# Attention C and D by query blocks: queries prepared three units ahead, a third bank for the maxima, shift rows turned a step later, and half of D's far masks added by TensorE

## What is computed

```python
# C: each chunk of 64 queries sees a band of keys (itself and two chunks back), with T5 bias and a sink
oc = chunk_band_prompt(qc, kc, vc, C_BACK_CHUNKS, bias_c, sinks)

# D: the 256 best keys of every query, chosen by an index score
_, sel = lax.top_k(score, topk)
s = jnp.einsum('bqhd,bqjd->bhqj', q, ks).astype(F32) * (q.shape[-1] ** -0.5) + bias   # T5 bias
s = jnp.where(valid[:, None], s, NEG_INF)
p = jax.nn.softmax(s, axis=-1).astype(vs.dtype)
o = jnp.einsum('bhqj,bqjd->bqhd', p, vs)
```

## Time and profile before

| | us |
|---|---|
| median of 3 runs (4599.81 to 4607.68) | 4602.56 |
| the profiled execution, its own time | 4597.78 |
| its span in the trace | 4596.0 |
| PE busy over the span | 3885.7 (85%) |
| DVE busy | 2402.1 (52%) |
| ACT busy | 1543.8 (34%) |
| POOL busy | 676.7 (15%) |
| main loop of C, from the trace (3298 to 3538) | 240 |
| main loop of D (3600 to 4330) | 730 |

### The profile page before, as it was taken

One profiled execution on the slowest core, in us unless ns is written; L12 is line 12 of the kernel. 1 busy time (PEld: TensorE's weight loads), 2 busy tenths in 40 slices (PEclk: granted clock), 3 DMA queues, 4 the chain that ended last, 5 costly groups with the idle time before them and its releaser, 6 DMA issues. The chain is left out here.

```text
span 4596.0 us, 52423 instructions
## 1 busy us (share of the span) xinstructions
PE 3885.7 (85%) x18001; PEld 2683.2 (58%) x18001; DVE 2402.1 (52%) x5162; ACT 1543.8 (34%) x2330; POOL 676.7 (15%) x408
## 2 busy tenths in 40 slices
PE   5999999978878999997988887789576578889798
PEld 3789989956655656566846433334344345555376
DVE  6211111157765444433310999999655677777522
ACT  3101001024433333333300777860233233333332
POOL 3100000022202111103400000000111432111133
PEclk9999999989998999998999898899788699999899
DMA  5222121143324332204411111011312101000243
GB/s 184 62 74 73 64 71 68 65 109 81 82 61 98 71 65 62 61 9 178 153 69 52 40 60 50 30 53 68 95 55 73 53 29 32 23 24 5 83 142 132
DMA packets 222647, 328.50 MB, mean 71 GB/s; under 512 B 22240, under 2 KB 129176, under 8 KB 221040
## 3 DMA queue, kind: packets, MB, share of 16 engines
q1 hardware_dynamic: 162768, 216.87, 16.8%
q10 hardware_dynamic: 54432, 91.91, 5.4%
q0 software_dynamic: 5216, 16.70, 1.7%
HBM read 214.42 MB, written 110.99 MB: 71 GB/s over the span
## 5 line engine op out<-in xcount | busy, mean ns | idle before, releaser
L2305 DVE TENSOR_SCALAR_CACHE_REDUCE cd_junk<-score,cd_thr 128x384 bf16<-128x384 f32 (+7 forms) x340 | 397.7, 1235 | 0.1
L1102 DVE TENSOR_REDUCE attB_mx<-attB_p_s 128x1 f32<-128x512 f32 (+2 forms) x360 | 211.3, 608 | 326.8 <-PE attB_p_s L949 209.8
L497 DVE COPY ab_stage<-ab_pA 128x256 f32<-128x256 f32 (+1 forms) x108 | 56.4, 522 | 601.1 <-PE ab_pA L466 571.5
L2345 ACT ACTIVATE cd_scratch<-score,cd_less 128x1664 bf16<-128x1664 f32 (+4 forms) x160 | 303.2, 1895 | 72.5 <-DVE cd_less L2324 67.0
L369 PE MATMUL cd_pA<-hT_cd,cd_W 128*128 128x512 f32 (+1 forms) x640 | 263.9, 577 | 74.0 <-ACT cd_stage L2451 61.5
L464 PE MATMUL ab_pA<-ab_W_hi,h_hi 128*128 128x256 f32 x1088 | 309.1, 284 | 3.3 <-PE ab_pA L466 3.2
L465 PE MATMUL ab_pA<-ab_W_lo,h_hi 128*128 128x256 f32 x1088 | 308.0, 283 | 0.0
L466 PE MATMUL ab_pA<-ab_W_hi,h_lo 128*128 128x256 f32 x1088 | 307.9, 283 | 0.0
L1575 PE MATMUL attD_p_o<-attD_pt,attD_v 128*65 128x512 f32 x548 | 296.4, 623 | 0.3
L1014 PE MATMUL attB_p_o<-attB_pt,attB_v 128*65 128x512 f32 (+3 forms) x656 | 287.5, 527 | 0.0
L495 ACT ACTIVATE ab_stage<-ab_pA 128x256 f32<-128x256 f32 (+1 forms) x108 | 50.0, 463 | 697.9 <-PE ab_pA L466 667.5
(11 more groups left out here) (378 smaller groups left out, 9294.0 us busy)
## 6 DMA issues: line engine op xcount, KB each, us to landing
t_qg<-cd_stage ACTq DMA_DIRECT2D x74, 256.0 KB, 2.0
ab_W_raw<-in_w_ab SPq DMA_DIRECT2D x17, 1024.0 KB, 5.8
mix_o<-t_o SPq DMA_DIRECT2D x34, 512.0 KB, 4.3
t_q<-ab_stage ACTq DMA_DIRECT2D x40, 256.0 KB, 2.0
t_k<-ab_stage ACTq DMA_DIRECT2D x40, 256.0 KB, 2.0
attA_raw<-t_k SPq DMA_DIRECT2D x16, 640.0 KB, 7.3
attA_raw<-t_q SPq DMA_DIRECT2D x16, 640.0 KB, 12.6
attB_raw<-t_k SPq DMA_DIRECT2D x16, 640.0 KB, 7.4
```

What stands on the lines that cost most here:

```text
L1102: nc.vector.tensor_reduce(out, src, AX.X, ALU.max).then_inc(s_free, 1)
L2305: nc.vector.tensor_scalar(junk[n % 2][:, 0:w], sc[n][:], T[:, n:n + 1], None, op, ALU.add, accum_out=cnt[:, n:n + 1]).then_inc(counted, 1)
L2345: nc.scalar.activation(scratch[:, 0:w], sc[n][:], ACT.Sign, bias=less[:, k:k + 1], accum_out=cnt[:, n:n + 1]).then_inc(signed, 1)
```

## The change

The plan and the instruction lists of `attention_by_blocks` change in four ways.

- **Queries ahead.** ACT's `round_queries(b)` and POOL's `prepare(b)` move from one step before the block's first fills to `due[u - 3]`, three units ahead. DVE's `split_queries(b)` gets a place of its own, two steps behind that (`split_at`). The `near_t` part of `prepare` becomes `add_near(b)`, at `due[u]`. The buffers (`NQ` = 3, two `q_raw`) stay.
- **Banks.** `p_s` has 3 banks (a fill waits for the reader of the bank three uses back) and `p_t` 2: `scores(c + 2)` waits for the reader of chunk `c`, before it was chunk `c - 1`.
- **Rows.** `shift_row(u)` and `keep_row(u)` move from `due[u] + 1` to `due[u] + 2`, and within a step ahead of masks and fills.
- **Masks by PE.** In D, chunks with an even key tile that is not one of the two nearest (128 of 306) get their mask by a third matmul into `p_t` (identity by the turned mask, 512 columns of bf16). ACT takes their exponent straight from `p_t`; DVE does nothing for them. `by_dve` and `biased` count the rest.

```diff
+        self.by_dve = [t >= self.chunks[self.chunks_of[u][-1]][1] - 1 or t % 2 == 1 for u, t in self.chunks]
+        self.biased = [sum(self.by_dve[:c + 1]) for c in range(len(self.chunks))]
...
-            self.rows_at[due[u] + 1].append(u)
+            self.rows_at[due[u] + 2].append(u)
...
-                self.blocks_at[max(begin - 1, 0)].append(b)
-        self.early_blocks = sorted({self.units[u][0] for u in self.early})
+                if b not in self.early_blocks:
+                    self.blocks_at[max(due[u - 3], 0)].append(b)
+                    self.split_at[max(min(due[u - 3] + 2, begin - 1), 0)].append(b)
+                    self.near_at[due[u]].append(b)
...
-        p_s = [ps(f"p_s{k}") for k in pair]
-        p_t = [ps(f"p_t{k}") for k in range(3)]
+        p_s = [ps(f"p_s{k}") for k in range(3)]
+        p_t = [ps(f"p_t{k}") for k in pair]
...
-            if g >= 2:
-                last = plan.order[g - 2]
+            if g >= 3:
+                last = plan.order[g - 3]
...
-                    if c >= 3:
-                        pe.wait_ge(t_biased, c - 2)
+                    if c >= 2 and plan.by_dve[c - 2]:
+                        pe.wait_ge(t_biased, plan.biased[c - 2])
+                    elif c >= 2:
+                        pe.wait_ge(exped, c - 1)
...
-                    nc.tensor.matmul(out, lo[:, ks], q_b[s][:, hs, :], start=False, stop=True).then_inc(t_done, 1)
+                    done = nc.tensor.matmul(out, lo[:, ks], q_b[s][:, hs, :], start=False, stop=plan.by_dve[c])
+                    if not plan.by_dve[c]:
+                        pe.wait_ge(mask_kept, plan.masks_before[b + 1])
+                        done = nc.tensor.matmul(out, identb[:], msk_t[b % 2][:, t * P:(t + 1) * P].unsqueeze(1).broadcast_to([P, GROUP, P]),
+                                                start=False, stop=True)
+                    done.then_inc(t_done, 1)
...
                 for c in range(NT):
                     exponent(c)
-                    for b in plan.blocks_at[c]:
-                        if b not in plan.early_blocks:
-                            round_queries(b)
-                    for b, k in plan.masks_at[c]:
-                        keep_mask(b, k)
                     for u in plan.rows_at[c]:
                         keep_row(u)
                         if kind == "C":
                             exp_sinks(u)
+                    for b in plan.blocks_at[c]:
+                        round_queries(b)
+                    for b, k in plan.masks_at[c]:
+                        keep_mask(b, k)
```

More of the change, by code:

```diff
@@ L1244, in __init__ @@
         self.blocks_at = [[] for _ in range(NT)]
+        self.split_at = [[] for _ in range(NT)]
+        self.near_at = [[] for _ in range(NT)]
         turns = lambda b: range(-(-self.tiles[b] // CHUNK_TILES)) if kind == "D" else range(0)
+        self.early_blocks = sorted({self.units[u][0] for u in self.early})
         for u in range(len(self.early), len(self.units)):
@@ L1270, in __init__ @@
         for c in range(NT):
+            order += [("row", u) for u in self.rows_at[c]]
             order += [("mask", b, k) for b, k in self.masks_at[c]] + [("fill", f) for f in self.fills_at[c]]
-            order += [("row", u) for u in self.rows_at[c]]
         self.use = {x: n for n, x in enumerate(order)}
@@ L1445, in prepare, with add_near @@
                             ).then_inc(near_q, 1)
[L1446 to L1454, removed]
+                def add_near(b):
+                    pool.wait_ge(mask_kept, plan.masks_before[b + 1])
+                    if b >= 2:
+                        pool.wait_ge(t_biased, plan.biased[chunks_of_block(b - 2)[-1]])
+                    for n in range(2 - off(b)):
+                        t = plan.tiles[b] - 1 - n
+                        done = nc.gpsimd.tensor_tensor(
+                            near_t[b % 2][:, n], bias_t[:, n],
+                            msk_t[b % 2][:, t * P:(t + 1) * P].unsqueeze(1).broadcast_to([P, HEADS, P]), ALU.add)
+                    done.then_inc(near_k, 1)
                 pool.wait_ge(fixed, FIXED)
@@ L1470, in _ @@
                     prepare(b)
+                for b in plan.early_blocks:
+                    if kind == "D":
+                        add_near(b)
                 if kind == "C":
@@ L1480, in _ @@
                             subtract_sinks(u)
+                    for b in plan.blocks_at[c]:
+                        prepare(b)
+                    if kind == "D":
+                        for b in plan.near_at[c]:
+                            add_near(b)
             @block.tensor
@@ L1492, in turn_bias @@
                     for n in range(4):
-                        bank = (p_t + [p_x])[n]
+                        bank = (p_t + p_o)[n]
                         for y in range(4):
@@ L1532, in fill @@
                         hi, lo, k0 = operands(x, b, a)
-                        out, ks = p_s[bank % 2][:, at * P:(at + n) * P], slice(k0 * P, (k0 + n) * P)
+                        out, ks = p_s[bank % 3][:, at * P:(at + n) * P], slice(k0 * P, (k0 + n) * P)
                         nc.tensor.matmul(out, q_a[s][:, h, :], hi[:, ks], start=(y == 0), stop=False)
@@ L1542, in shift_row @@
                     for i in range(GROUP):
-                        done = nc.tensor.matmul(p_s[g % 2][0:AUX, i * P:(i + 1) * P], shift[u % 2][:, i, :], ident_r[:],
+                        done = nc.tensor.matmul(p_s[g % 3][0:AUX, i * P:(i + 1) * P], shift[u % 2][:, i, :], ident_r[:],
                                                 start=(i == 0), stop=(i + 1 == GROUP))
@@ L1604, in _ @@
                         scores(c + 2)
+                    for u in plan.rows_at[c]:
+                        shift_row(u)
                     for b, k in plan.masks_at[c]:
@@ L1608, in _ @@
                         fill(f)
-                    for u in plan.rows_at[c]:
-                        shift_row(u)
                     values(c)
@@ L1653, in exponent @@
                 def exponent(c):
-                    act.wait_ge(t_biased, c + 1)
+                    if plan.by_dve[c]:
+                        act.wait_ge(t_biased, plan.biased[c])
+                    else:
+                        act.wait_ge(t_done, c + 1)
                     if c >= NPT:
                         act.wait_ge(valued, c - NPT + 1)
-                    nc.scalar.activation(pt[c % NPT][:], s_t[c % NST][:], ACT.Exp).then_inc(exped, 1)
+                    src = s_t[plan.biased[c] % NST] if plan.by_dve[c] else p_t[c % 2]
+                    nc.scalar.activation(pt[c % NPT][:], src[:], ACT.Exp).then_inc(exped, 1)
                 def keep(u):
@@ L1815, in _ @@
                     negate(u)
-                add_bias(0)
-                add_bias(1)
+                for c in range(2):
+                    if plan.by_dve[c]:
+                        add_bias(c)
                 for c in range(NT):
-                    if c + 2 < NT:
+                    if c + 2 < NT and plan.by_dve[c + 2]:
                         add_bias(c + 2)
-                    for b in plan.blocks_at[c]:
-                        if b not in plan.early_blocks:
-                            split_queries(b)
+                    for b in plan.split_at[c]:
+                        split_queries(b)
                     for f in plan.fills_at[c]:
```

28 lines of the change are left out of this document (13 added, 15 removed).

## The result

The changed kernel takes **4576.58 us**, the median of 5 runs (4571.57 to 4580.28), against 4602.08 us for the kernel before in 5 runs on the same chip: a ratio of 0.9939 with a 95% interval of 0.9928 to 0.9951, 25.5 us faster. The forecast was 59.5 us faster, 4543 us. The direction and the range held; less than half of the gain came.

What follows compares the result with a forecast made beforehand. PE was taken to bound both loops, losing time to stops and the low clock behind them. D's terms sum to −84.5 us and C's to +25, together −59.5, giving 4543 us, range 4500 to 4597.

Steps and rivals of the forecast that it cites:

- The stops for split queries in D (−68 and −31 of low clock): D, blocks 4 to 16: 13 PE stops go, 68.0 us idle and 31 us of low clock behind them.
- I cost this at nothing: D: DVE is held 1.4 us, then splits for 1.2; PE can go on meanwhile, so no cost.
- small waits where DVE comes late: D: a new cost of 5 us.
- The load of block 4 (+5): D: block 4's query load stands behind `store(0)`, costing 5 us once.
- PE can go on without DVE for about two steps, 3.6 us: D: PE's reserve from three banks of maxima and chunks already biased.
- Rival 5: D: DVE's split, held by `near`, still stops PE, 70 us in 13 blocks; 4613 us in all, chance 0.12.
- case 1: The prediction's own case: D gains its stops and C gets slower; 4543 us, chance 0.58.
- The rows (−17.5): D: shift-row waits go, 17.5 us, since the row stands a step later and needs a bank read earlier.
- The masks by PE (+30): D: 128 more matmuls of 0.24 us each on PE, 30 us more, bounds 0 and 55.
- it was not the bound, so that gains nothing by itself: D: DVE loses 128 mask sums, with no gain because DVE does not bound the loop.
- C (+25): C: loads behind a store lengthen the block period from 15.54 to 17.9 us; 25 us slower, bounds 0 and 45.
- C loses its stops altogether: Rival in C: needs loads ahead of outputs, ruled out by SP order; 94 us off C, 4424, chance 0.03.

Runs made afterwards that it cites:

- experiment 5: Changed kernel with D's query rounding and POOL's preparation two steps later and DVE's split six steps behind them instead of two: 4527.16 us.
- experiment 1: Changed kernel with each store on the SP queue one block later: 4466.22 us.
- 10: Kernel of number 9 with the rows turned one step earlier, at `due[u] + 1` as before the change: 4410.60 us.
- number 9: Changed kernel with stores one block later, D's preparation and `near_t` two steps later, split six steps behind preparation, every mask by DVE: 4409.24 us.
- 11: Kernel of number 9 with two banks `p_s` for maxima and three `p_t` for scores, as before the change: 4435.53 us.
- 12: Kernel of number 9 with both banks and rows as before the change: 4438.87 us.
- experiment 8: Kernel of experiment 5 with every mask added by DVE, no third matmul: 4508.02 us.
- experiment 4: Changed kernel with every mask in D added by DVE, no third matmul: 4576.0 us.

## Why the prediction was wrong, point by point

- **The stops for split queries in D (−68 and −31 of low clock): right for blocks 6 to 16.** At blocks 4 and 5 the moved split is itself held (6.88 and 7.84 us) and PE stops behind it. Once the new holds are taken away too (experiment 5), D's loop comes to 646.7 us, where the terms of the prediction give 727.6 − 80.5 = 647.1. That this agrees so closely is luck: terms that are off cancel within the sum, see the load, the rows and the early blocks below.
- **The step that failed** is "I cost this at nothing", together with the 5 us for "small waits where DVE comes late". It asked how long the *split* is still held, and found it short; indeed 11 splits of the steady blocks came near 1.22 us. It did not ask which other DVE instruction would now run beside POOL's 6.9 us. That one was `negate`'s cast, 61.9 us in 30, and it cost 39 us of the loop in blocks 5 to 14 (experiment 5). The forecast was off by 34 in all: 47 more in D, 4 less in C, 6 less ahead of C, 1 more behind D, and 5 less because the median did not lie above the profiled execution as it had before (that execution, of 4576.58 us with a span of 4574.8, is the median).
- **The load of block 4 (+5): too small.** It cost about 10 us at block 1 (8.7 by experiment 1, 10.1 by experiment 5).
- **"PE can go on without DVE for about two steps, 3.6 us": near, but the holds are longer.** A held cast of 5.82 us stopped PE for 3.31 us, where an `add_bias` came late, and one of 4.52 us for 1.09 us, at a turned row. That is a reserve of 2.5 and of 3.4 us (an estimate, the hold less the stop), and the prediction had put the hold at 2.6. Rival 5 had the mechanism, a hold under `near` that drains PE's reserve, but on the split, where it came true in two blocks, and at 70 us; the time lies between it and case 1.
- **The rows (−17.5): of two reasons one holds.** The later step gives nothing (10 against 9), the third bank does: 26.3 us of the time (11 against 9), and with the rows 20.8 us of D's loop (652.0 in 12 against 631.2 in 9). This was measured with every mask on DVE and the holds cleared, not in the changed kernel itself.
- **The masks by PE (+30): right where PE is the bound,** 29 us of matmuls, 19 us of the whole (experiment 8). In the changed kernel they cost nothing on balance (experiment 4), since "it was not the bound, so that gains nothing by itself" does not hold behind a held cast.
- **C (+25): right.** +21.1, in 13 stops of up to 7.4 us, and the period 17.2 us (3404.32 to 3421.55 at PE's stops) against the forecast 17.9. But the prediction named the cause, loads behind a store in SP's queue, and gave "C loses its stops altogether" 0.03, since the SP order ruled it out. That is so for this change; a move of three lines in that order gives 110 us (experiment 1).
- **What stays open.** The first blocks of D (2 to 7) still stop PE, for instance 6.97 and 6.18 us in number 9, where units have too few steps to hold POOL's passes apart; no run tried to remove these. D's loop is 6 us longer in number 9 (631.2) than in experiment 8 (624.9), and the traces put 6.1 of it in blocks 2 to 4 (75.1 against 69.0): there block 4's preparation, whose load is no longer late, falls on a cast of 7.99 us that took 0.17 in experiment 8.

## What to carry to other kernels

When an instruction moves in time, list not only what it needs and who needs it, but what will run beside it: here GpSimd's passes over SBUF held the VectorE casts, splits and subtractions that met them, and a cast of four columns was the costly one. Look at each in-order DMA queue for the transfer that stands behind a store: its place in the queue can matter more than the step at which it is issued. And a hand-over of work from one engine to another is judged after the stalls are gone, since before that it may only pay for them.

## What the runs showed of the hardware

- A VectorE cast of 128x4, 0.17 us by itself, can be held over several GpSimd instructions in a row. The longest in number 9, in the timeline of block 4's preparation:

```profile
3535.20 2.84 POOL L1443 TENSOR_SCALAR attD_q_b<-attD_q_a,attD_only_q 66x1024 fp32r<-66x1024 f32 x1 [11.44 <-ACT attD_q_a L1651]
...
3536.21 7.99 DVE L1775 CAST attD_shift<-attD_nm 128x4 fp32r<-128x4 f32 x1
3538.01 4.07 POOL L1450 TENSOR_TENSOR attD_near<-attD_bias,attD_msk 128x2048 f32<-128x2048 f32 x1
3542.05 4.19 POOL L1461 TENSOR_TENSOR attD_near_t<-attD_bias_t,attD_msk_t 128x1024 f32<-128x1024 f32 x2
```

It starts within the copy and ends at 3544.20, two instructions further, in the middle of the third row, whose 4.19 us are two passes. The page "SBUF — State Buffer" of the Trainium skill (Who interferes with whom) states that casts and copies of VectorE can take the port pair that it shares with GpSimd, and that the one that is first keeps it for its whole instruction. By that rule the trace agrees for one instruction; no run here shows why VectorE does not get its turn between two. Between the two passes of `near_t` it does: in experiment 5 a cast ends 0.03 us behind the first pass (which the trace ends at 3962.19), and the subtraction behind it is held by the second:

```profile
3960.05 4.24 POOL L1461 TENSOR_TENSOR attD_near_t<-attD_bias_t,attD_msk_t 128x1024 f32<-128x1024 f32 x2 [10.75 <-ACT attD_msk_t L1660]
...
3961.95 0.27 DVE L1775 CAST attD_shift<-attD_nm 128x4 fp32r<-128x4 f32 x1
3962.25 2.06 DVE L1777 TENSOR_TENSOR attD_shift<-attD_nm,attD_shift 128x4 fp32r<-128x4 f32 x1
```

- Not everything on VectorE is held. In the changed kernel's timeline above the `TENSOR_REDUCE` of 3970.93 ran in 0.17 us within GpSimd's copy, and in experiment 5 sums and maxima that read PSUM took their usual time under both passes:

```profile
3943.43 0.69 DVE L1760 CUSTOM_DVE_ANT_0 attD_junk<-attD_p_s,attD_msk 128x512 bf16<-128x512 f32 x1 [1.32 <-PE attD_p_s L1550]
...
3945.23 4.08 POOL L1450 TENSOR_TENSOR attD_near<-attD_bias,attD_msk 128x2048 f32<-128x2048 f32 x1
3945.74 0.68 DVE L1760 CUSTOM_DVE_ANT_0 attD_junk<-attD_p_s,attD_msk 128x512 bf16<-128x512 f32 x1
```

- With PE's 90 us of stops in C gone, the loop was 104 us shorter; the same 762 matmuls took 165 us of busy time at a granted clock of 0.80 and 142 at 0.96.
